# Prologue of a two-block kernel: modulation in pieces of columns, latents by row panels, position bias read in a narrower form

## What is computed

```python
cond = jax.nn.silu(c)                                            # c: (1, 1024)
mod = (cond @ w_ada + b_ada)[:, None, :]                         # w_ada: (1024, 6*1024)
sh1, sc1, gt1, sh2, sc2, gt2 = jnp.split(mod, 6, axis=-1)
h = rmsnorm(x, g_mix) * (1 + sc1) + sh1                          # x: (1, 256, 1024)
proj = h @ w_in                                                  # (1024, 4640)
a_qkv, c_q, c_kv, k_r, gate_a, gate_b = split(proj)              # 1536, 768, 256, 32, 1024, 1024
y_a = dilated_attention(a_qkv, rel_bias) @ w_up_a                # 8 heads, bias by distance
y_b = mla(c_q, c_kv, k_r, positions, g_q_lora, w_uq, ...) @ w_up_b
x = x + gt1 * ((sigmoid(gate_a) * y_a + sigmoid(gate_b) * y_b) @ w_o)
x = x + gt2 * swiglu(rmsnorm(x, g_ffn) * (1 + sc2) + sh2)
# second block: a mixer with 4 heads of sparse attention that use rel_bias_2, and a second swiglu
```

## Time and profile before

| | us |
|---|---|
| median of 3 runs | 855.09 (854.41 to 855.58) |
| profiled execution, device time | 855.07 |
| its span | 853.3 |
| TensorE busy | 809.9 (95%) |
| VectorE busy | 544.8 (64%) |
| ScalarE busy | 453.9 (53%) |
| GpSimd busy | 61.6 (7%) |
| mean granted TensorE clock | 0.937 of 2.4 GHz |

### The profile page before, as it was taken

How to read it: one execution, slowest core, us unless ns; L and a number is a source line. 1 busy time by engine, 2 the same in 40 slices (tenths; PEclk the granted TensorE clock), 3 DMA queues, 4 the chain that set the end, 5 groups by cost and what they waited for, 6 DMA issues and landing times.

```text
span 853.3 us, 14553 instructions
## 1 busy us (share of the span) xinstructions
PE 809.9 (95%) x5316; PEld 728.3 (85%) x5316; DVE 544.8 (64%) x1012; ACT 453.9 (53%) x857; POOL 61.6 (7%) x94
## 2 busy tenths in 40 slices
PE   3989999999899999999999999979998999999998
PEld 2679998798799789999999898968797999999997
DVE  2785426978769686666666674548857666666663
ACT  3455436666464565555554556167945555555552
POOL 7000002000035500000000020000000000000000
PEclk9579989999879999999999989679997999999999
DMA  8789856878649656666666566503215556565631
GB/s 271 241 223 304 267 150 184 278 216 253 200 127 303 178 148 198 196 177 194 179 189 182 118 162 166 155 26 100 75 51 147 163 173 200 172 197 176 197 100 50
DMA packets 187181, 151.07 MB, mean 177 GB/s; under 512 B 13298, under 2 KB 170408, under 8 KB 187008
## 3 DMA queue, kind: packets, MB, share of 16 engines
q1 hardware_dynamic: 181728, 143.61, 57.8%
q10 hardware_dynamic: 3760, 5.87, 1.9%
q0 software_dynamic: 1648, 1.00, 0.6%
HBM read 146.78 MB, written 3.41 MB: 176 GB/s over the span
## 4 chain that ended last, share of the span: by engine, by line
PE 83%; DVE 9%; ACT 3%; DMA 2%; issue 2%; ACTq 0%; DVEq 0%
PE ps L1898 19%; PE ps L1591 13%; PE ps L1592 13%; PE ps L1593 13%; PE ps L1900 10%; DVE w_lo L1052 3%; PE ps L1707 2%; PE ps L1975 1%; PE ps L1831 1%; DMA arena<-in_x 1%; PE ps L1666 1%; PE ps L1639 1%; PE ps L1809 1%; DVE sq L1109 1%; DVE sq L1135 1%
## 5 line engine op out<-in xcount | busy, mean ns | idle before, releaser
L1052 DVE TENSOR_TENSOR w_lo<-raw,w_hi 128x1024 fp32r<-128x1024 f32 (+3 forms) x223 | 270.3, 1233 | 99.1 <-ACT w_hi L660 98.8
L1898 PE MATMUL ps<-h,w_hi 128*128 128x512 f32 x704 | 254.1, 400 | 2.7 <-DVE h L1131 1.7
L660 ACT ACTIVATE w_hi<-raw 128x1024 fp32r<-128x1024 f32 (+3 forms) x223 | 226.6, 1038 | 32.2 <-PE ps L1593 11.1
L1900 PE MATMUL ps<-h,w_lo 128*128 128x256 f32 x704 | 199.6, 283 | 0.0
L1898 PEld LDWEIGHTS ps<-h,w_hi 128*128 128x128 f32 x704 | 133.3, 189 | 36.6 <-issue 3.3
L1591 PE MATMUL ps<-h,w_hi 128*128 128x256 f32 (+1 forms) x472 | 139.8, 296 | 6.8 <-ACT bias L950 1.9
L1592 PE MATMUL ps<-h,w_hi 128*128 128x256 f32 (+1 forms) x472 | 135.6, 287 | 0.0
L1593 PE MATMUL ps<-h,w_lo 128*128 128x256 f32 (+1 forms) x472 | 135.4, 287 | 0.0
L1900 PEld LDWEIGHTS ps<-h,w_lo 128*128 128x128 f32 x704 | 133.4, 189 | 0.0
L1591 PEld LDWEIGHTS ps<-h,w_hi 128*128 128x128 f32 (+1 forms) x472 | 91.8, 194 | 12.6 <-issue 9.1
L1591 PE MATMUL ps<-g_hi,w_hi 128*128 128x256 f32 x352 | 98.6, 280 | 0.0
(11 more groups left out here) (330 smaller groups left out, 1168.1 us busy)
## 6 DMA issues: line engine op xcount, KB each, us to landing
raw<-in_w_in SPq DMA_DIRECT2D x53, 512.0 KB, 5.3
raw<-in_w_ada SPq DMA_DIRECT2D x48, 512.0 KB, 4.7
raw<-in_w_down SPq DMA_DIRECT2D x44, 512.0 KB, 4.3
raw<-in_w_gate_up SPq DMA_DIRECT2D x44, 512.0 KB, 4.0
raw<-in_w_gate SPq DMA_DIRECT2D x22, 512.0 KB, 4.0
raw<-in_w_up SPq DMA_DIRECT2D x22, 512.0 KB, 5.1
raw<-in_w_o SPq DMA_DIRECT2D x8, 512.0 KB, 4.6
raw<-in_w_out SPq DMA_DIRECT2D x8, 512.0 KB, 3.5
```

The source lines that it names most:

```text
L660: A(w_hi[:, m % HL, 0:w], raw[:, n % RAW, 0:w], ACT.Copy).then_inc(hi_done, 1)
L1052: V.tensor_tensor(w_lo[:, m % HL, 0:w], raw[:, n % RAW, 0:w], w_hi[:, m % HL, 0:w].bitcast(f32), sub).then_inc(lo_done, 1)
L1898: T.matmul(bank[:, :], hi, h2[:, k, :, :].rearrange("p a b -> p (a b)"), start=(k == 0), stop=False, skip_group_check=True)
L1900: ins = T.matmul(bank[:, 0:SEQ], lo, h_hi[:, k, :], start=False, stop=(k == KC - 1), skip_group_check=True)
```

## The change

Modulation: the two terms (scale and shift) of the same channels are loaded side by side, in five pieces of 256, 256, 256, 128 and 128 channels. A panel holds two k (four in the two last pieces) of both terms and is loaded by two DMAs, with rows of 1 KB (512 bytes in the two last pieces). VectorE adds even and odd k into two accumulators, in instructions of 512 (256) columns, each of which waits for the one before the last. TensorE sums a piece (`mod_sums`), VectorE makes gain and shift of these channels, scales them, and ScalarE and VectorE write the two parts of h.

Latents: instead of column chunks over all k, row panels: panel k holds the 1024 latent columns of 128 rows of `w_in`, and TensorE adds its products into eight regions of four PSUM banks (`lat_panel`). The panels of piece q - 1 are multiplied after the sums of piece q. The order of the loads follows. The squares, high and low parts of the latents are made between the chunks kr, aq and ak.

The squares for the norm are taken by ScalarE from x before its transposition, with the sum over the channels in the same instruction; VectorE's total and TensorE's sums go. The rotary angles are computed on VectorE after all pieces, and ScalarE's sine and cosine come after them, ahead of the splits from kr on.

Position bias: two products make one row per head on 8 and 4 partitions; two DMAs write them to DRAM, one DMA copies them to 16 rows, and eight DMAs of 16 partitions each read them back, 256 columns per head instead of 384, four ahead of the value copies and four behind them. For the first query block the scores read the last 128 columns instead of a copy of them.

The diff, cut to its core:

```diff
...
+ROWS = 16
+PIECES = ((0, 2), (2, 4), (4, 6), (6, 7), (7, 8))
+AHEAD_OF = ((), (0, 1), (2, 3), (4, 5), (6,), (7,))
...
-    for m in range(ADA_FIRST):
-        ada(m, -1)
-    for c in range(6):
-        chunk("cq", w_in, C_CQ + c * P)
-    for c in range(2):
-        chunk("ckv", w_in, C_KV + c * P)
+    mod_panels, mod_count = [], [0]
+    def ada_piece(q):
+        a, b = PIECES[q]
+        w = (b - a) * P
+        kn = PW // (2 * w)
+        for k in range(0, KC, kn):
+            directs.append((len(splits) - 1, [(0, kn, 2 * w, at_, w, cols(I["w_ada"], g * D + a * P, w, k, kn))
+                                              for at_, g in ((0, 1), (w, 0))]))
+            mod_panels.append((q, k, kn, 2 * w))
+            mod_count.append(mod_count[-1] + kn)
+    for q in range(len(PIECES) + 1):
+        for k in AHEAD_OF[q]:
+            panel("lat%d" % k, [(0, 1, D, 0, D, cols(w_in, C_CQ, D, k, 1))])
+        if q < len(PIECES):
+            ada_piece(q)
+    assert len(mod_panels) == ADA_FIRST
+    mods_of = [[m for m in range(ADA_FIRST) if mod_panels[m][0] == q] for q in range(len(PIECES))]
...
+        LAT_ORDER = (0, 2, 4, 6, 1, 3, 5, 7)
+        def lat(c):
+            return ps[c // 2][:, SEQ * (c % 2):SEQ * (c % 2) + SEQ]
...
+                        sp.wait_ge(*((mod_step, mod_count[order[o] + 1]) if order[o] < ADA_FIRST else
+                                     (ada_used, order[o] + 1 - ADA_FIRST) if order[o] < ADA else
...
+            arrived(act, "in_x")
+            for t in range(TT):
+                line(A(sq[:, 4 * t:4 * t + 4, :].rearrange("p a b -> p (a b)"), x_tm[:, t, :], ACT.Square,
+                       accum_out=small[:, 68 + t:69 + t]))
+            act.wait_ge(s("const_ready"), 1)
+            line.settle()
+            line(A(rms, small[:, 68:70], ACT.Sqrt, scale=1.0 / D, bias=eps_c), "rms_ready")
...
+            act.wait_ge(s("frow_mm"), 2)
+            line(A(bias[0:A_HEADS, 0, :], ps[0][0:A_HEADS, 0:FW], ACT.Copy))
+            line(A(bias[0:NSA_HEADS, 1, :], ps[1][0:NSA_HEADS, 0:FW], ACT.Copy), "frow_copied")
+            act.wait_ge(s("vb_t"), 1)
+            line(A(vb[:, :], ps[2][:, 0:VB_ROWS], ACT.Copy), "vb_ready")
+            for q, (a, b) in enumerate(PIECES):
+                split.ahead(AHEAD_OF[q + 1][-1] - AHEAD)
+                act.wait_ge(s("shift_ready"), q + 1)
+                for c in range(a, b):
+                    high(0, c, shift=0)
             act.wait_ge(s("arg_ready"), 1)
             line(A(sinT[:, :, :], ang, ACT.Sin))
             line(A(cosT[:, :, :], arg, ACT.Sin, scale=-1.0, bias=hpi_c), "trig_ready")
-            act.wait_ge(s("vb_t"), 1)
-            line(A(vb[:, :], ps[2][:, 0:VB_ROWS], ACT.Copy), "vb_ready")
-            split.ahead(-1)
-            highs(0, shift=0)
-            act.wait_ge(s("h_lo"), 8)
-            for c in range(8):
-                l = (L["cq"] + L["ckv"])[c]
-                split.ahead(outputs[l])
-                await_out(act, l)
-                line(A(sq[:, c, :], lin(l), ACT.Square), "lat_sq")
-                line(A(mix_hi[:, c, :], lin(l), ACT.Copy, scale=vcol("g_q_lora", c)), "lat_hi")
-                if c == 1:
-                    act.wait_ge(s("frow_copied"), NB)
-                    act.dma_start(frow_dram, bias[:, :, :].rearrange("p a b -> p (a b)")).then_inc(s("frow_out"), 16)
+            act.wait_ge(s("frow_copied"), 1)
+            act.dma_start(rows_dram[0:A_HEADS, :], bias[0:A_HEADS, 0, :]).then_inc(s("row_out"), 16)
+            act.dma_start(rows_dram[A_HEADS:NB, :], bias[0:NSA_HEADS, 1, :]).then_inc(s("row_out"), 16)
+            split.ahead(nth("kr") - 2)
+            def latent_high(n):
+                c = LAT_ORDER[n]
+                act.wait_ge(panel_used, nth("lat%d" % (KC - 1)) + 1)
+                if n >= 4:
+                    act.wait_ge(s("lat_lo"), n - 3)
+                line(A(sq[:, c, :], lat(c), ACT.Square), "lat_sq")
+                line(A(mix_hi[:, c, :], lat(c), ACT.Copy, scale=vcol("g_q_lora", c)), "lat_hi")
+            latent_high(0)
...
+                if c < 7:
+                    latent_high(c + 1)
...
+                if c == 0:
+                    act.wait_ge(s("row_out"), 32)
+                    act.dma_start(frow_dram, bass.AP(rows_dram.tensor, 0, [[0, ROWS], [1, NB * FW]])).then_inc(s("frow_out"), 16)
+            def read_bias(r0, r1):
+                act.wait_ge(s("frow_out"), 16)
+                for r in range(r0, r1, ROWS):
+                    act.dma_start(bias[r:r + ROWS, :, P:FW],
+                                  bass.AP(frow_dram.tensor, P - 1 - r, [[NB * FW - 1, ROWS], [FW, NB], [1, SEQ]]))\
+                        .then_inc(s("bias_in"), 16)
             split.ahead(nth("av", 3))
+            read_bias(0, P // 2)
             for t, l in enumerate(L["av"]):
                 await_out(act, l)
                 line(A(a_v[:, t, :], lin(l, 512), ACT.Copy), free_name(l))
+            read_bias(P // 2, P)
...
+            def mod_part(m):
+                n, (q, k0, kn, w) = direct_of[m], mod_panels[m]
+                dve.wait_ge(raw_in[n % RAW], raw_count[n])
+                if k0 == 0 and q >= 2:
+                    dve.wait_ge(s("mod_mm"), q - 1)
+                for j in range(kn):
+                    k = k0 + j
+                    src, dst = raw[:, n % RAW, j * w:(j + 1) * w], mod_acc[:, q % 2, k % 2, 0:w]
+                    if k < 2:
+                        ins = V.tensor_scalar(dst, src, cond[:, k:k + 1], None, mult)
+                    else:
+                        dve.wait_ge(mod_step, mod_count[m] + j - 1)
+                        ins = stt(out=dst, in0=src, scalar=cond[:, k:k + 1], in1=dst, op0=mult, op1=add)
+                    ins.then_inc(mod_step, 1)
+            def gain_shift(q):
+                a, b = PIECES[q]
+                dve.wait_ge(s("mod_mm"), q + 1)
+                line(V.tensor_tensor(mod[:, 1, a:b], GAIN[q][:, a:b], va[:, KC + a:KC + b], add))
+                line(V.tensor_tensor(mod[:, 0, a:b], SHIFT[q][:, a:b], va[:, a:b], add), "shift_ready")
+                line.settle()
+                line(stt(out=gs[:, 0, a:b], in0=mod[:, 1, a:b], scalar=1.0, in1=va[:, 48 + a:48 + b], op0=add, op1=mult))
+            def scaled(c):
+                line.settle()
+                line(stt(out=sq[:, c, :], in0=xT[:, c, :], scalar=gs[:, 0, c:c + 1], in1=NRM, op0=mult, op1=mult), "h_ready")
+            def low0(c):
+                dve.wait_ge(s("h_hi"), c + 1)
+                line.settle()
+                line(stt(out=h_lo[:, c, :], in0=sq[:, c, :], scalar=mod[:, 0, c:c + 1], in1=h_hi[:, c, :].bitcast(f32),
+                         op0=add, op1=sub), "h_lo")
+            def rotary_angles():
...
+            dve.wait_ge(s("va_ready"), 1)
             dve.wait_ge(s("cond_ready"), 1)
-            for m in range(2 * KC):
-                ada(m)
-                if m < KC:
-                    total(m, 0)
-                if m == KC:
+            def scaled_piece(q):
+                gain_shift(q)
+                for c in range(*PIECES[q]):
+                    scaled(c)
+                split.ahead(AHEAD_OF[q + 1][-1] - AHEAD)
+            def low_piece(q):
+                for c in range(*PIECES[q]):
+                    low0(c)
+            for q, ms in enumerate(mods_of):
+                half = len(ms) // 2
+                for m in ms[:half]:
+                    mod_part(m)
+                if q == 1:
+                    dve.wait_ge(s("x_copied"), 4)
+                    dve.wait_ge(s("inv_ready"), 1)
+                if q >= 1:
+                    scaled_piece(q - 1)
+                for m in ms[half:]:
+                    mod_part(m)
+                    if q >= 1 and m == ms[half]:
+                        low_piece(q - 1)
+                if q == 0:
                     inverse(0)
-            split.ahead(-AHEAD)
-            modulate(0, 2)
-            line(stt(out=gs[:, 0, :], in0=mod[:, 1, :], scalar=1.0, in1=va[:, 48:56], op0=add, op1=mult))
+            scaled_piece(len(PIECES) - 1)
+            low_piece(len(PIECES) - 1)
+            rotary_angles()
...
+            for n, l in enumerate(L["kr"] + L["aq"] + L["ak"][0:3]):
+                c = LAT_ORDER[n]
                 split.ahead(outputs[l])
-                dve.wait_ge(s("lat_hi"), c + 1)
-                line(stt(out=mix_lo[:, c, :], in0=lin(l), scalar=vcol("g_q_lora", c), in1=mix_hi[:, c, :].bitcast(f32),
-                         op0=mult, op1=sub), free_name(l))
+                dve.wait_ge(s("lat_hi"), n + 1)
+                line(stt(out=mix_lo[:, c, :], in0=lat(c), scalar=vcol("g_q_lora", c), in1=mix_hi[:, c, :].bitcast(f32),
+                         op0=mult, op1=sub), "lat_lo")
...
+            def mod_sums(q):
+                a, b = PIECES[q]
+                pe.wait_ge(mod_step, mod_count[mods_of[q][-1] + 1])
+                if q >= 2:
+                    pe.wait_ge(s("shift_ready"), q - 1)
```

(40 more changed lines are left out.)

106 lines of the change are left out of this document (46 added, 60 removed).

## The result

Over 20 runs of each kernel on one chip the changed kernel takes 848.43 us (845.69 to 854.64) against 857.4 us (854.41 to 862.62): the ratio is 0.9897, with an interval of 0.9883 to 0.9911, some 9 us. The profiled executions lie closer together: 849.46 us (span 847.3) against 855.07 us (span 853.3), 5.6 us. A single execution of either kernel can lie several us from the median, so I read positions from profiles and sizes from medians. Beside the profile after I show a second one of the same kernel (e0), because the two differ by 2.1 us at my anchor, the copy of the first query projection (aq, chunk 0) on ScalarE.

What follows compares the result with a forecast made beforehand. TensorE's queue behind the eight latent products was taken to bound the kernel; start, middle and end brought the aq 0 copy from 83.1 to 75.7, so 855.07 - 7.4 = 847.7 us, range 841 to 853.5.

Steps and rivals of the forecast that it cites:

- wait in front of kr: TensorE, done with panel 7 at 68, idles about 2 us until the late rotary angles and kr's split finish at 70.3.
- rival 2: Load of x at the start: x lands at about 11, the start moves up 3.3 us, 844.4 us; chance 0.24.
- sums of piece 0: TensorE at the start: eight one-column products of 0.22 us at full clock, from 18.0 to 19.8 us.
- price of 1.12 per bias product: TensorE's bias rows at the start: 13.48 / 12 = 1.12 us each, two products, done at 22.8.
- last load of piece 2: SyncE's queue: behind latent panels 2 and 3, at 1.5 us per panel, the last of six lands at 37.4.
- near tie: Latent loop: VectorE ends piece 2 at 43.2, behind TensorE's 42.7 by 0.5 us.
- rival 3: Slot loop: short rows in two parts load slower, piece 2 and the clock come 2.7 us later, 850.4 us; chance 0.16.
- these stand behind in its program: ScalarE makes the high parts of latent panels 0 and 1 only after the bias and vector block copies, by 25.8.
- Loss of the clock at panels 2 and 3: TensorE in the latent loop: clock taken as lost, panels 2 and 3 take 7.5 us, to 52.6.
- Rival 1: TensorE's latent panels: the clock never comes back, every burst stays at half clock, 867.9 us; chance 0.07.
- more than 1 us of change there: After the aq 0 copy: nothing gained or lost; the forecast is wrong if this time changes by over 1 us.
- granted clock 0.5 from about 22 to 38: Sign in the profile after: TensorE at half clock then and again for 4 us from 45, else full.

Runs made afterwards that it cites:

- e1: The kernel before with only the narrow position bias: two products instead of twelve, rows through DRAM, eight reads; 851.07 us, ratio 0.9932.
- e7: e1 with 4 MB of extra DRAM transfers added at the places of the old ones; 852.30 us, ratio 0.9956 to the kernel before.
- e10: The kernel before with only the rotary angles moved behind the scaled h, sine and cosine behind the high parts of h; 861.52 us, ratio 1.0047.
- e8: The changed kernel with each modulation panel loaded as one transfer with 4 KB rows, from wrong columns; 847.04 us, ratio 0.9865 to the kernel before.
- e5: The changed kernel with nine idle-keeping products added in front of the sums of piece 1; 848.42 us, ratio 0.9901 to the kernel before.
- e3: The changed kernel with latent panel splits made earlier: high parts ahead of the bias copies, low parts one step sooner; 842.08 us, ratio 0.9833 to before.
- e9: The changed kernel with the rotary angles put back at the head of VectorE; 850.26 us, ratio 0.9918 to the kernel before.
- e6: e3 with five idle-keeping products in front of the sums of piece 1 and none behind the latent panels; 840.73 us, ratio 0.9803 to the kernel before.
- e4: The changed kernel without the idle-keeping products in the latent loop; 846.84 us, ratio 0.9879 to the kernel before.
- e11: e6 with one idle-keeping product behind latent panels 0 and 1; 839.11 us, ratio 0.9781 to the kernel before.
- e2: The changed kernel with the wide position bias restored: twelve products and two wide reads; 861.93 us, ratio 1.0065 to the kernel before.

## Why the prediction was right, and where it wasn't

The time was right: 847.7 forecast, 848.43 measured, and a shift of 7.4 us at the anchor against 5.3 and 7.4 in the two profiles. The absolute time fits better than the gain, though: I started from 855.09, a median of three, and taken side by side over 20 executions the kernel before has 857.4, so that the change is worth 9.0 us and not 7.4. The path to the time was partly wrong, and that two errors cancelled is luck.

| step (end, us) | forecast | after | e0 |
|---|---|---|---|
| first accumulation starts | 10.4 | 11.3 | 9.6 |
| piece 0 on VectorE | 15.3 | 18.0 | 16.8 |
| factor spread | 20.6 | 22.7 | 21.5 |
| low parts of panels 0 and 1 | 27.0 | 29.8 | 28.5 |
| sums of piece 1 | 34.2 | 37.1 | 35.9 |
| panels 0 and 1 | 41.7 | 45.1 | 44.2 |
| sums of piece 2 start | 43.2 | 46.9 | 45.2 |
| panels 2 and 3 | 52.6 | 56.0 | 52.8 |
| sums of piece 4 | 61.8 | 65.8 | 63.6 |
| panel 7 | 68 | 72.2 | 70.1 |
| wait in front of kr | 2.3 | 0 | 0 |
| anchor | 75.7 | 77.9 | 75.7 |

**The start.** That x, the squares and the root would set the reciprocal (18.4) was right within the spread (17.9 and 16.7), and x came 1.3 us sooner than before (13.0 against 14.3), 1.3 of the 3.3 us of my rival 2. Its condition holds: TensorE starts on x at 11.5 to 13.0 us in all nine profiles with the short rows, at 14.1 to 14.4 in before, e1, e7 and e10, and at 14.2 in e8, with 4 KB rows; that packets are the reason is not shown. In the profile after it brought nothing, because TensorE then waited 1.43 us for piece 0, whose third panel landed 11.9 us after its issue. The mis-sized term is the sums of piece 0. I priced them at 8 x 0.22 = 1.8 us, full pace, though the earlier trace rows gives 3.55 for as many records at half clock; they took 3.54 (in e5 1.92, with the same program up to there, so either pace can occur). With 0.4 us more for spreading the factor and 0.6 for the two bias products (2.8 against 2.24) this makes 2.7 us. The price of 1.12 per bias product was an average over two paces: in the kernel before the first eight records took 2.86 us and the other sixteen 10.61, 0.72 and 1.33 us per product, so that not all twelve ran at half clock, as I had read. The 2.7 us arrive undiminished at the low parts of panels 0 and 1 and, through the slots, at every later load.

**The middle.** The mechanism was right: SyncE issues in order, piece 2 stands behind panels 2 and 3, and these wait for the low parts. I had the last load of piece 2 at 37.4; its second panel came at 38.15, and transfers went on until 40 to 41 us (share 0.49 in 39 to 40, 0.13 in 40 to 41, 0.00 in 41 to 42), later by what the low parts were late. But I read the meeting of VectorE and TensorE as a near tie (0.5 us of waiting on TensorE) and kept the slower loop as a rival that needs slow loads (rival 3). e3 and e8 show that the loads needn't be slow: the loop is slow by the place of the splits. Undoing this is worth 5.5 us (e3, by medians), which I didn't see when I wrote down that "these stand behind in its program" and went on.

**The clock.** Panels 0 and 1 took 8.2 us instead of 7.5: the pace came up 5.3 us after the first latent product (36.94 to 42.2; in e0 6.1), not 4.3, and a full-pace product of a row panel comes every 0.118 us, not 0.113. Loss of the clock at panels 2 and 3 was right for one profile and wrong for the other. Rival 1 (the clock never comes back) fell: panels 4 to 7 run at full pace in every profile of the changed kernel. The Trainium skill, "TensorE: Matmul & The Clock Gate", section "Loop structure matters more than you think", makes a wait for a transfer between bursts the case where the engine goes cold each time. The traces agree in part: the clock fell behind waits of 0.77 us (after and e9), 0.31 (e6), 1.63 (e4), 1.72 (e8) and 4.74 (e5) in front of the sums of piece 2 and stayed up where there was none (e0, e3, e11), but it also stayed up over 1.37 us in front of the shorter sums of piece 3 (e0).

**The end.** The wait of 2 us in front of kr was the wrong step. From the end of the sums of piece 4 to kr's low part I had counted 8.5 us (61.8 to 70.3). It took 6.2 (65.75 to 71.95), and 6.2 again in e0 and e4, while TensorE needs 6.5 from there to the end of panel 7. Lines of VectorE and ScalarE:

```profile
65.78 0.16 DVE L1156 TENSOR_TENSOR mod<-ps,va 128x1 f32<-128x1 f32 x1 [2.29 <-PE ps L1753]
...
67.34 1.28 ACT L746 ACT_TABLE_LOAD   x1
...
71.52 0.43 DVE L1093 TENSOR_TENSOR w_lo<-raw,w_hi 128x256 fp32r<-128x256 f32 x1 [0.81 <-ACT w_hi L684]
```

VectorE took about what I had priced (angles 68.17 to 70.3). The step that I had wrong is the one behind it, 3.5 us from the angles to kr's low part, where 1.7 were measured: the table load of 1.28 us, which I had put behind the angles, ran at 67.34, while ScalarE waited for them, and the two DMA issues (0.29 and 0.31 us) ran beside sine and cosine. So kr's low part was done 0.3 us before TensorE needed it. That TensorE came 4.2 us later than forecast, at 72.2, is not the reason: VectorE itself waits for the sums of piece 4 (2.29 us), so a late TensorE moves both. e4 is the test: without the 0.86 us of idle-keeping products ahead of panel 7, TensorE waits 0.49 us there. The late TensorE (+4.2, in e0 +2.1) and the missing wait (-2.3) cancel in e0 and by half in the profile after, and this is why the sum held.

**Behind the anchor.** I said that more than 1 us of change there would be wrong, and it was, in e0: 7.4 us at the anchor become 9.9 at the gates (144.8 before, 134.9) and 6.7 at the end. In the profile after they are 5.3, 6.3 and 6.0. The eight issues of the position bias use up ScalarE's slack and no more: its idle time before the latent root is 0.25 us, where it was 2.21. What differs along with these positions is the clock at the changes of stage: e0 has no window at half clock from 90 to 140 us, before has it from 117 to 124, after from 114 to 118. Farther back, ScalarE's root at 487.4 us of before (L889) stands 9.0 us sooner in e0, 17.4 in e6 and 18.3 in e11, and its copy at 577.3 us in the second block (L801) 5.1, 13.5 and 18.3: up to 3.9 us are lost or kept in between, in a stretch that no part of the change touches. What decides it is open; it is as large as the scatter of single profiles about the medians.

**Parts.** By e1 and e2 the narrow bias is worth 2 to 5 us in the old order and 12 to 14 us in the new one, so the parts don't add: pieces, row panels, early squares and late angles without it are 0.65% slower than before, all together 1% faster. The late rotary angles are worth nothing that could be measured here (e9) and cost 4 us alone (e10).

## What to carry to other kernels

Where loads are issued in order into a ring of slots, look for the instruction that frees the slot and for everything that stands ahead of it in its engine's program; moving that instruction ahead of unrelated work (e3) brought 5.5 us on top of the 9 of the whole change, while faster loads (e8) and a faster TensorE (e5) brought nothing that could be measured. Only with the ring out of the way did the clock and the idle-keeping products bring a gain clear of the noise (e11 against e3). And a part should be priced with its neighbours: the same twelve products cost 12 to 14 us or 2 to 5, and the same moved wait 4 us or nothing, by what stands behind it.

## What I had not expected of the hardware

The granted clock of a window can read 1.00 while products come at half pace. Windows of the changed kernel: busy, instructions, granted clock, DMA.

```profile
38.00:39.00 1.00, 1.00 (x6) 1.00 (x6) 0.85 (x2) 0.00 (x0) 0.00 (x0) 1.00 1.10 352
43.00:44.00 1.00, 1.00 (x11) 1.00 (x10) 1.00 (x3) 0.00 (x0) 0.00 (x0) 1.00 0.82 172
50.00:51.00 1.00, 1.00 (x6) 1.00 (x6) 0.39 (x2) 0.00 (x0) 0.00 (x0) 0.50 0.84 246
```

A window counts every product that touches it: six of one shape at a record of 0.50 (50 to 51) and also at one of 1.00 (38 to 39), and eleven once the pace has come up, at 42.2 us. In the kernel before, windows with products at half pace read 0.50 from 22 to 41 us. So the rise of the mean granted clock from 0.937 to 0.958 overstates the gain, and my sign "granted clock 0.5 from about 22 to 38" could not have shown: the windows read 1.00 there, with products 0.213 us apart. The spacing of equal products is the surer reading. That the two disagree after an idle stretch is what the traces show; why, they don't. The Trainium skill, "TensorE: Matmul & The Clock Gate", section "Seeing it yourself", warns that the clock events in a trace have been seen to be unreliable and wants them checked against something else; by these rows the trace agrees.

Short rows of loads cost at the start and not later. With 1 KB rows the third modulation panel landed 11.9 us after its issue, and from 10 to 22 us the queues moved 344 to 381 GB/s at a DMA share of 1.05 to 1.10; with 4 KB rows (e8) they moved 391 to 419 GB/s from 10 to 20 us, and VectorE had no wait in piece 0. The same change of rows left the wait of piece 2, 3.26 us, at 3.28, though the DMA share was 1.03 to 1.09 there as well (34 to 38 us). The latent panels ahead of it in the queue have 4 KB rows in both kernels; whether that is the reason, no run tells.
